# Reordering the expert loop of a two-block model kernel, with single bias rows and longer runs of weights

## What is computed

```python
mod = c_act @ w_ada[l] + b_ada[l]
shift, scale, gate = jnp.split(mod, 3, axis=-1)
h = rms_norm(x, norm_g[l]) * (1.0 + scale[:, None, :]) + shift[:, None, :]
proj = h @ w_in[l]
...
def expert_block(args):
    xb, e = args
    hid = jax.nn.silu(xb @ w_gate[e]) * (xb @ w_up[e])
    return hid @ w_down[e]
...
contrib = (ys[dest] * sw[:, None]).astype(h.dtype)
out = jnp.zeros((m, d), h.dtype).at[stok].add(contrib)
...
x = x + g_f * y
return rms_norm_2(x, final_norm_g)
```

## Time and profile before

| | us |
|---|---|
| median of 3 runs (1517.9 to 1522.44) | 1522.38 |
| the profiled execution | 1521.11 |
| its span, first to last instruction | 1519.4 |
| TensorE busy | 1321.9 (87%) |
| VectorE busy | 592.7 (39%) |
| ScalarE busy | 347.4 (23%) |
| GpSimd busy | 170.2 (11%) |
| mean granted TensorE clock | 0.932 |

### The profile page before, as it was taken

The page is one execution under the profiler, slowest core; times in us unless marked ns, Lnnn a source line. Parts: engine busy times, 40 slices in busy tenths (PEclk is TensorE's granted clock), DMA queues, the critical chain, the costliest instruction groups (busy, mean ns, idle before and its releaser), DMA issues.

```text
span 1519.4 us, 21160 instructions
## 1 busy us (share of the span) xinstructions
PE 1321.9 (87%) x7554; PEld 659.6 (43%) x7555; DVE 592.7 (39%) x1109; ACT 347.4 (23%) x741; POOL 170.2 (11%) x276
## 2 busy tenths in 40 slices
PE   4989999998999999999779995788888888888891
PEld 1445656568744444464354454333233333333330
DVE  1466373744123333496675735122122211221214
ACT  1222232321244422212353421001101011011012
POOL 3011111111110000000000000111111111111102
PEclk8999999999999999999799996799999999899896
DMA  9252707061271100223100484369999999899974
GB/s 325 96 195 48 246 17 269 9 195 31 65 213 44 42 1 0 74 70 83 42 1 0 149 349 180 114 221 394 400 404 407 410 403 404 352 404 402 406 308 185
DMA packets 112864, 302.38 MB, mean 199 GB/s; under 512 B 10778, under 2 KB 67250, under 8 KB 91792
## 3 DMA queue, kind: packets, MB, share of 16 engines
q1 hardware_dynamic: 103488, 285.12, 50.3%
q0 software_dynamic: 9296, 16.17, 3.6%
HBM read 297.75 MB, written 13.73 MB: 205 GB/s over the span
## 4 chain that ended last, share of the span: by engine, by line
PE 77%; DVE 9%; DMA 6%; issue 3%; DVEq 2%; ACT 2%; POOL 1%; SPq 0%; POOLq 0%; ACTq 0%; PEldq 0%
PE bank L814 22%; PE bank L2672 17%; PE bank L2688 8%; PE bank L745 7%; PE bank L860 4%; PE bank L823 3%; DMA arena<-in_w_ada 2%; PE bank L803 2%; DVE hT L2766 1%; DVE hT L2764 1%; DMA yT<-xn_scratch,idx_col 1%; DMA arena<-in_ada_w 1%; DVEq L2525 1%; DMA expert_rows<-cactB,place_col 1%; PE bank L1042 1%
## 5 line engine op out<-in xcount | busy, mean ns | idle before, releaser
L814 PE MATMUL bank<-hT,arena 128*128 128x512 f32 x768 | 339.4, 599 | 0.0
L2672 PE MATMUL bank<-arena,hT 128*64 128x512 f32 x1024 | 257.4, 661 | 55.3 <-DVE hT L2766 55.3
L814 PEld LDWEIGHTS bank<-hT,arena 128*128 128x128 f32 x768 | 144.7, 191 | 180.1 <-issue 177.3
L2672 PEld LDWEIGHTS bank<-arena,hT 128*64 128x64 f32 x1024 | 78.4, 152 | 213.8 <-issue 168.1
L745 PE MATMUL bank<-arena,yT 128*128 128x512 f32 x256 | 114.5, 602 | 2.3 <-DVE yT L1615 2.3
L2772 DVE TENSOR_SCALAR hT<-hT 128x256 f32<-128x256 f32 x32 | 9.4, 294 | 273.2 <-ACT hT L2731 273.2
L2688 PE MATMUL bank<-arena,yT 128*64 128x512 f32 x512 | 115.4, 592 | 0.6 <-ACT yT L2739 0.6
L2731 ACT ACTIVATE hT<-bank 128x256 f32<-128x256 f32 x32 | 12.3, 384 | 327.0 <-PE bank L2672 327.0
L745 PEld LDWEIGHTS bank<-arena,yT 128*128 128x128 f32 x256 | 48.2, 192 | 60.6 <-issue 56.3
L860 PEld LDWEIGHTS bank<-arena 64*64 64x64 f32 x1856 | 59.5, 135 | 28.4 <-issue 14.4
L860 PE MATMUL bank<-arena 64*64 64x64 f32 x1856 | 64.1, 220 | 7.0 <-POOLq L655 4.5
(11 more groups left out here) (452 smaller groups left out, 1577.7 us busy)
## 6 DMA issues: line engine op xcount, KB each, us to landing
...
```

The lines of the kernel that those rows point to most:

```text
L814: last = T.matmul(bank[0:rows, :], w[:, k, 0:rows], hT[:, k, :], start=k == 0, stop=k == KD - 1)
L2672: last = T.matmul(banks[1 + ub][MT * h:MT * h + MT, :], tile.xT[:, k, :], wgu[u][:, :, k, 256 * h:256 * h + 256], start=k == 0, stop=k == ...
```

## The change

In the expert loop each engine's list is written in another order. TensorE turns the rows of e+1 right behind gate/up of e, ahead of down of e-1; VectorE makes its two passes over them between the clamp and hidden's products. GpSimd gathers rows two steps ahead, and so expert 1's rows too before the loop. Expert 0's extra tiles are done in step 1, behind gate/up of expert 1. Within an extra tile, the next extra tile's rows are turned behind its gate/up. SyncE asks for gate and up of e+1 ahead of down of e. The weights of gate and up are laid out side by side on the host, so one load of 2 MB for each half, with 16 KB runs; down's weights too come in 16 KB runs, and chunks of `w_in` in runs of 4 KB. The modulation's bias comes as single rows, the first ahead of GpSimd's constants. The two small loads `w2` and `a2` move behind the first projection's chunk, and no longer wait. The final gain comes as one row before the loop; TensorE spreads it by a matmul with ones, ScalarE copies it, and VectorE does all four products.

```diff
@@ sp_block1
             load_ada(KD)
-            sp.wait_ge(s_ada_used, KD - 2)
-            sp.dma_start(w2sb[0:64, :], A["w2"]).then_inc(s_small, 16)
-            sp.dma_start(w2sb[64:128, :], A["a2"]).then_inc(s_small, 16)
...
-                    sp.dma_start(ring[:, n % NRING], c[0][:, :, c[1]:c[1] + P]).then_inc(ring_sem[n % NRING], 16)
+                    sp.dma_start(ring[:, n % NRING], chunks[n]).then_inc(ring_sem[n % NRING], 16)
...
+                if name == ("proj", 0, 1):
+                    sp.dma_start(w2sb[0:64, :], A["w2"]).then_inc(s_small, 16)
+                    sp.dma_start(w2sb[64:128, :], A["a2"]).then_inc(s_small, 16)
@@ pool_block1
+                src = bass.AP(b.tensor, at * 512, [[512, m], [1, 512]])
+                eng.dma_start(ada_bias[0:32 * m:32, :], src).then_inc(s_adaw, 16)
...
             done = pool.done
+            done(G.memset(ada_bias, 0.0))
+            bias_load(0)
             done(G.memset(ones, 1.0))
...
-                src = bass.AP(b.tensor, at * 512, [[512, m], [0, 32], [1, 512]])
-                eng.dma_start(ada_bias[0:32 * m, :], src).then_inc(s_adaw, 16)
@@ which extra tiles a step does
+        def extras_due(e):
+
+            if isinstance(e, int) and e < 2:
+                return (0, 1) if e else ()
+            return (e,)
@@ sp_experts
+            def load_gate_up(u, e):
+                for half in range(2):
+                    eng.dma_start(wgu[u][:, half, :, :, :], A["w_gu"][bass.ds(e, 1), :, half, :, :, :]
+                                  .rearrange("o p a k n -> (o p) a k n")).then_inc(w_gu[u][half], 16)
...
+            def next_gate_up(u, e):
+
+                n = extras_before(e - 2)
+                eng.wait_ge(first.gate_up, e - 1)
+                stand_alone(eng)
+                eng.wait_ge(more_.gate_up, n + 1)
+                stand_alone(eng)
+                load_gate_up(u, e)
+
             def body(it, u, e):
...
+                if not (isinstance(e, int) and e == NE - 1):
+                    next_gate_up(after(it, u)[1], e + 1)
+                n = extras_before(e - 2)
+                eng.wait_ge(first.down, e - 1)
+                stand_alone(eng)
+                eng.wait_ge(more_.down, n + 1)
+                stand_alone(eng)
+                load_down(u, e)
@@ pool_experts
-                if not (isinstance(e, int) and e == NE - 1):
-                    it1, u1 = after(it, u)
-                    eng.wait_ge(tiles[u1].xf, it1 + 1)
-                    gather(tiles[u1], u1, e + 1, s_picked[0], e + 1)
-                extras(eng, e, more)
-                if not (isinstance(e, int) and e == 0):
+                if not (isinstance(e, int) and e >= NE - 2):
+                    it2, u2 = after(*after(it, u))
+                    eng.wait_ge(tiles[u2].xf, it2 + 1)
+                    gather(tiles[u2], u2, e + 2, s_picked[0], e + 2)
+                due = extras_due(e)
...
-            eng.wait_ge(tiles[0].xf, 1)
-            gather(tiles[0], 0, 0, s_picked[0], 0)
+            for u in range(2):
+                eng.wait_ge(tiles[u].xf, 1)
+                gather(tiles[u], u, u, s_picked[0], u)
...
-            eng.dma_start(finalG, bass.AP(A["final_g"].tensor, 0, [[0, P], [1, DM]])).then_inc(s_ld, 16)
-            eng.wait_ge(s_ld, 16)
-            for t in range(POOL_ROWS):
-                eng.wait_ge(s_scaled, t + 1)
-                done(G.tensor_tensor(yg[:, 2 * t, :], yg[:, 2 * t + 1, :], finalG, MUL))
-                eng.sem_inc(s_rows_pool, 1)
@@ pe_experts
                 gate_up(tiles[u], first, u, e, u, it)
-                if not begun:
-                    finish(it0, u0, e - 1)
-                overflow(it, u, e)
                 if not (isinstance(e, int) and e == NE - 1):
                     it1, u1 = after(it, u)
                     turn_rows(tiles[u1], first, e + 1, it1)
+                due = extras_due(e)
+                if len(due) == 2:
+                    overflow(it, u, e, due[0])
+                if not begun:
+                    finish(it0, u0, e - 1)
+                if due:
+                    overflow(it, u, e, e)
...
+            for half in range(2):
+                last = T.matmul(banks[2 * half + 1][:, :], ones_row, gain_row[:, 512 * half:512 * half + 512], start=True, stop=True)
@@ dve_experts
             def body(it, u, e):
+                clamped(tiles[u], first, e)
+                if not (isinstance(e, int) and e == NE - 1):
+                    it1, u1 = after(it, u)
+                    rows_in(tiles[u1], first, e + 1, it1)
                 hidden(tiles[u], first, u, e)
@@ lay_out
-        "w_gate": a["w_gate_2"][0], "w_up": a["w_up_2"][0], "w_down": a["w_down_2"][0],
+        "w_gu": np.stack([a[n][0].reshape(NE, P, 2, KD // 2, FE) for n in ("w_gate_2", "w_up_2")], axis=3),
+        "w_down": a["w_down_2"][0].reshape(NE, FE // P, P, DM).transpose(0, 2, 1, 3),
```

198 lines of the change are left out of this document (102 added, 96 removed).

## The result

The changed kernel takes 1498.42 us (median of 4 runs, 1497.02 to 1505.34), the kernel before 1522.41 beside it (4 runs, 1517.9 to 1524.87). The ratio is 0.9834, with a 95% interval of 0.98 to 0.9868: about 24 us, 1.6 to 1.7%, faster, and the interval leaves 20 to 30. The forecast was 1489 in a range of 1479 to 1511.

The account below looks back on a forecast made before the run. The prediction took TensorE and DMA as nearly level, with the weight stream binding after the change; start -3.7, loop -26.2 and end -2.6 summed to -32.5 us, from 1521.1 to 1489 us, range 1479 to 1511.

Parts of the forecast that it names:

- The bound: Expert loop: TensorE and DMA within 2 us of each other; steps shorten to 12.3 us, then the weight stream binds.
- The start: Before the loop: single bias rows land the eighth weight slice 4.8 us earlier; in sum -3.7 us.
- The extra gather's 2.1 us: Ahead of the loop: a second gather on GpSimd before the extra tile's first delays gate/up 0 by 2.1 us.
- The stream's start: Loop's begin: expert 3's weights are asked for at 992.3 us, before the start's gain, and the stream doesn't stop.
- The rate: Expert loop's weight loads: longer runs save 0.45 us an expert, from 16.46 to 16.0 us, 13 us in all.
- straight line through two windows: Weight loads: windows of 4 KB runs (406 GB/s) and 8 KB runs (426) extended to 435 GB/s for 16 KB.
- Rival B: Expert loop's weight loads: run length gives nothing, 13 us more, 1502 us; chance 0.24.
- The last landing: End of the weight stream: 29 experts x 16.0 = 464 us after 992.3, so 1456.3 us.
- The end: After the last matmul: GpSimd's products and the late gain load go; -2.6 us, bounds 0 and -4.
- C, the clock: Expert loop: TensorE, waiting for weights, runs partly at 1.2 GHz and falls back; +24 us, 1513; chance 0.13.
- D, long packets slowed by rows: Expert loop: long packets hurt the stream beside gathers and scatters; 59 us with the lost gain, 1548; chance 0.08.
- E: The change doesn't do what it says: cover fails, stream held at its start, runs give nothing; 1515 to 1522; chance 0.07.

Follow-up runs that it names:

- the bias rows' experiment: Changed kernel with the modulation's bias loaded repeated over 32 partitions, both loads behind GpSimd's constants, as before: 1507.09 us, ratio 0.9894.
- before with long runs alone: Kernel before with gate, up and down weights in 16 KB runs, the loop's order old: 1527.95 us, ratio 0.9996.
- changed again: The changed kernel as it is, timed a second time: 1502.37 us, ratio 0.9854.
- rows spread: Changed kernel with a tile's rows at places 0, 4, 8 and so on, to even out the DMA engines: 1501.58 us, ratio 0.9851.
- short runs: Changed kernel with the experts' weights in the old layout, gate and up in 8 KB runs, down in 4 KB: 1504.82 us, ratio 0.9883.
- old order of asking: Changed kernel with SyncE asking for weights one expert after the other, nothing ahead of a down: 1506.46 us, ratio 0.9911.
- turning late: Changed kernel with the next rows turned, and VectorE's passes over them made, at a step's end: 1505.28 us, ratio 0.9874.
- extras in step 0: Changed kernel with expert 0's extra tiles worked on in step 0, ahead of gate/up 1: 1493.49 us, ratio 0.9809.
- expert 4 asked for first: Changed kernel with SyncE asking for expert 4's gate and up ahead of expert 3's, before its loop: 1494.58 us, ratio 0.9799.

## Why the prediction was right, and where it was not

**The bound.** Right. The wait for VectorE turned into one for weights, a plain early step is 12.0 to 12.8 us (12.3), TensorE's lead is spent at expert 14 (forecast: step 14) and again at 25 (24), and the end follows the stream. Turning the rows late again brings all 55 us of wait back, and costs 3 to 6 us by the ratios, 10 to 13 by the one profile.

**The start.** The mechanism is right to 0.2 us at the slice (4.8 worked out, 5.0 by the bias rows' experiment, 5.9 between the kernels). The first matmul of the projections (L824 in the changed kernel) begins at 38.3 us instead of 41.5, and in the other profiles with the new start at 36.3 to 38.3: 3.2 to 5.2 earlier, 3.7 were forecast. At the loop it is less: the gather of expert 0 is issued 1.9 us earlier, so part of the term is lost on the way. By L824's matmuls it is still 3.1 us at the middle (480 us) and 2.1 at their end (847.5); no run shows why. The extra gather's 2.1 us are there: the rows of the extra tile are turned at 960.77 and gate/up 0 begins at 961.81, unchanged from the earlier trace rows; the prediction had 960.2. That before and after can be compared at all to 2 us here is luck: the clock's stretch in 360 to 390 us would have moved either by 6.

**The stream's start.** 989.75 against 992.3 - 3.7 = 988.6: 1.2 us late.

**The rate.** The total is right and its reason is not. An engine's mean is 16.05 us an expert, 16.0 were forecast, but the long runs gave 0.07 to 0.19 us and not 0.45. The base of 16.46 was too high: it was taken to the last landing of the kernel before, which lies 3.7 us behind the engines' mean. Taken to the mean it is 16.46 - 3.7 / 28.33 = 16.33. The straight line through two windows had read 20 GB/s of difference, and one of them lay beside rows and the other not. Rival B's price (run length gives nothing) is nearer to the truth than the forecast's; that the mean came out at 16.05 all the same is luck. The Trainium skill's figure of 512 B for line rate (page "DMA: Bandwidth & Descriptors", section "Specifications") would have made this term 0 of 13 us; the experiments show 2 to 6, nearer to the page than to my line.

**The last landing.** This is the step that failed: "29 experts x 16.0 = 464, last landing 992.3 + 464". It takes 16 engines for one. They end 1445.3 to 1464.3, and TensorE needs the last. 9.2 us of the 10.2 that the sum was off in the profiled execution are this. The count: stream start 1.2 late, rate 29 x 0.05 = 1.5, drift 9.2, less 0.5 of lag between landing and last matmul, is 11.4; the last matmul was forecast for 1460.5 - 3.7 = 1456.8 and ended at 1468.0, 11.2 later; the end gave back 1.0. The measured time lies in the stated range, but the range was not made for this: its upper part stood there for runs that give nothing and for a slower clock, and no rival had engines that drift apart. Nor can this kernel be measured to the 0.3% that was stated: the interval of the ratio is 0.34% to either side.

**The end.** Forecast -2.6, measured 29.1 against 32.7 us, -3.6. All of VectorE's steps are at 1.3 us, and the results land 4.75 us after they are asked for.

**What each part is worth.** Against the mean ratio of the two samples of the changed kernel (0.9844), undoing a part costs, in us of 1522: the order of asking 10, the bias rows 8, the runs 6, the early turning 5, each with an interval of 7 to 10 either way; the first extras behind the second gate/up cost 5 themselves. With 3.6 at the end, by the trace, that is 10 + 8 + 6 + 5 + 3.6 - 5 = 28 beside a measured 24. Only the order of asking is clear of nothing by this measure. The loop alone can be measured from the start of gate/up 0 to the last matmul, free of what happens ahead of it, with one profile for each kernel:

| kernel | us |
|---|---|
| before; before with long runs alone | 524.8; 526.0 |
| changed; changed again | 506.2; 509.3 |
| same loop: rows spread; old bias | 506.7; 508.1 |
| short runs | 511.6 |
| old order of asking | 514.6 |
| turning late | 519.7 |
| extras in step 0; expert 4 asked for first | 502.6; 502.3 |

By it the loop gained 16 to 19 us; undoing the runs costs 2 to 5, the order of asking 5 to 8, the early turning 10 to 13 (from the longest of its four executions). So the two measures don't agree on which of the last two is larger, and that stays open. The prediction had put the order of asking at nothing by itself ("both are long satisfied") and the gathers two steps ahead at a side effect. The first is a fifth to two fifths of the gain, and with the rows turned early but gathered one step ahead the kernel is 76 us slower than before.

**The rivals.** B, nothing from the runs: above. C, the clock: in part, and at no cost. TensorE's waits for weights were 22.6 us in 22 pieces and 22.3 in 16. Gate/up's matmuls are 600 ns on average, where they were 661, but down's are 649, where they were 592: some of the downs behind a wait for weights run in part at 1.2 GHz instead of 2.4, as in this row of the chain and the window over it (granted clock 0.68):

```profile
1429.28 5.38 PE bank L2720 x16
...
1429.30:1434.60 5.30, 5.30 (x17) 1.46 (x17) 0.67 (x2) 0.00 (x0) 0.00 (x0) 0.68 0.97 414
```

5.4 us is what C had put down for a down. But the stream leaves TensorE 16.0 - 12.3 = 3.7 us to spare in a step, gate/up mostly keeps the full clock, and over 1010 to 1310 us the granted clock rose from 0.93 to 0.95. The Trainium skill's HAM oscillation (page "TensorE: Matmul & The Clock Gate") describes tiles that each start at the low clock where their work is shorter than the wait for their load. This trace bears that out only in part: of the 14 downs of the main tiles behind a wait of 0.7 to 2.4 us, 5 took 5.3 to 5.4 us and 9 the usual 3.65, and gate/up took 7.7 to 8.7 us with the wait for its second half inside. D, long packets slowed by rows: that slowing is real, 16 KB packets took 616 ns without gathers and 639 beside them, but so it was with 8 KB (median 313, mean 323 in the loop before), and it had its price in the kernel before already. E: no.
